# Weights of the seven-product tiles 64 bytes further in their places, sums of activations back at byte 0, in a two-block float32 kernel

## The reference

```python
    u = rms_norm(h, g_mlp) @ w_ff1                 # 1024 -> 4096
    h = h + jnp.square(jax.nn.relu(u)) @ w_ff2     # 4096 -> 1024
```

## Time and profile before

| what | us |
|---|---|
| median of three timed runs | 2050.3 (2049.81 to 2050.95) |
| the profiled execution, its own time | 2047.93 |
| its span, first to last instruction | 2046.1 |
| TensorE busy | 1995.9 (98% of the span) |
| GpSimd busy | 990.6 (48%) |
| VectorE busy | 1353.9 (66%) |
| ScalarE busy | 924.9 (45%) |

### The profile page before, as it was taken

How to read it: one execution, slowest core, us unless ns; L and a number is a source line. 1 busy time by engine, 2 the same in 40 slices (tenths; PEclk the granted TensorE clock), 3 DMA queues, 4 the chain that set the end, 5 groups by cost and what they waited for, 6 DMA issues and landing times.

```text
span 2046.1 us, 28723 instructions
## 1 busy us (share of the span) xinstructions
PE 1995.9 (98%) x11012; PEld 1598.4 (78%) x11012; DVE 1353.9 (66%) x2302; ACT 924.9 (45%) x1533; POOL 990.6 (48%) x1205
## 2 busy tenths in 40 slices
PE   6999999999999999999999999999999999999998
PEld 3877676888888667668889898786776788898877
DVE  5366758988294579966766565466896585665634
ACT  4542434443232556784333333445578533333342
POOL 1344204876666325541567767302345147676740
PEclk9999999999999999999999999999999999999999
DMA  9034631332333211113232324322111313323331
GB/s 330 28 105 142 220 124 43 103 102 83 106 101 103 77 54 42 45 39 104 75 111 83 117 90 134 97 75 80 46 42 42 103 63 103 103 85 122 114 103 62
DMA packets 166809, 194.43 MB, mean 95 GB/s; under 512 B 8592, under 2 KB 159504, under 8 KB 163216
## 3 DMA queue, kind: packets, MB, share of 16 engines
q1 hardware_dynamic: 166096, 189.44, 27.8%
q10 hardware_dynamic: 576, 3.15, 0.4%
HBM read 190.48 MB, written 2.10 MB: 94 GB/s over the span
## 4 chain that ended last, share of the span: by engine, by line
PE 67%; DVE 18%; ACT 5%; POOL 4%; DMA 4%; issue 2%; SPq 0%; DVEq 0%; ACTq 0%; POOLq 0%
PE ps L865 12%; PE ps L867 12%; PE ps L866 12%; POOL wl L3069 3%; DMA ring<-in_ff_seven_dram 3%; PE ps L884 2%; PE ps L886 2%; PE ps L885 2%; PE ps L1305 2%; PE ps L1307 2%; PE ps L1306 2%; PE ps L912 2%; DVE mix L2697 2%; DVE acts L2699 2%; ACT wh L1542 2%
## 5 line engine op out<-in xcount | busy, mean ns | idle before, releaser
L3069 POOL TENSOR_TENSOR wl<-ring,wh 128x256 fp32r<-128x256 f32 x1008 | 781.4, 810 | 592.3 <-ACT wh L1542 591.5
L1542 ACT ACTIVATE wh<-ring 128x1024 fp32r<-128x1024 f32 (+3 forms) x394 | 338.4, 888 | 305.7 <-DMA ring<-in_ff_seven_dram 93.5
L865 PE MATMUL ps<-acts,wh 128*128 128x512 f32 x880 | 345.6, 393 | 1.8 <-POOL wl L3069 1.2
L867 PE MATMUL ps<-acts,wl 128*128 128x512 f32 x880 | 342.7, 389 | 0.0
L866 PE MATMUL ps<-acts,wh 128*128 128x512 f32 x880 | 342.5, 389 | 0.0
L865 PE MATMUL ps<-xh,wh 128*128 128x512 f32 (+1 forms) x592 | 233.8, 395 | 2.6 <-POOL wl L3069 2.6
L2625 DVE SCALAR_TENSOR_TENSOR mix<-ps,par,mix 128x441 f32<-128x441 f32 (+2 forms) x352 | 213.8, 686 | 29.2 <-ACT mix L1789 29.1
L866 PE MATMUL ps<-xl,wh 128*128 128x512 f32 (+1 forms) x592 | 231.2, 391 | 0.0
L867 PE MATMUL ps<-xh,wl 128*128 128x512 f32 (+1 forms) x592 | 231.2, 391 | 0.0
L865 PEld LDWEIGHTS ps<-acts,wh 128*128 128x128 f32 x880 | 165.1, 188 | 40.9 <-issue 5.4
L867 PEld LDWEIGHTS ps<-acts,wl 128*128 128x128 f32 x880 | 165.2, 188 | 34.9
(11 more groups left out here) (474 smaller groups left out, 4133.6 us busy)
## 6 DMA issues: line engine op xcount, KB each, us to landing
ring<-in_w_ff_dram SPq DMA_DIRECT2D x40, 1024.0 KB, 5.2
ring<-in_w_in_dram SPq DMA_DIRECT2D x28, 1024.0 KB, 5.1
ring<-in_ff_seven_dram SPq DMA_DIRECT2D x24, 1024.0 KB, 4.8
ring<-in_ffn_w_up_dram SPq DMA_DIRECT2D x22, 1024.0 KB, 4.9
ring<-in_w_ada_dram SPq DMA_DIRECT2D x17, 1024.0 KB, 5.0
ring<-in_w_out_dram SPq DMA_DIRECT2D x12, 1024.0 KB, 5.1
ring<-in_ffn_w_down_dram SPq DMA_DIRECT2D x8, 1024.0 KB, 5.0
ring<-in_w_ple_gate_dram SPq DMA_DIRECT2D x8, 1024.0 KB, 5.0
```

Source lines behind the costliest of these rows:

```text
L865: t.matmul(b[0:m, 0:n], s.hi[:, k, a:a + m], x2[0][:, k, :], start=k == ks[0], stop=False)
L867: i = t.matmul(b[0:m, 0:n], s.lo[:, k, a:a + m], x2[0][:, k, :], start=False, stop=k == ks[-1])
L1542: a.activation(s.high[hf], s.raw[hf], ACT.Copy).then_inc(*up("hi", "hi", name, hf))
L3069: i = p.tensor_tensor(lo, raw, hi.bitcast(F32), ALU.subtract)
```

## The change

The split weights of seven-product tiles begin 16 elements (64 bytes) into their places, in `wh` and in `wl`, which grow by 16 elements. All four sums of activations begin at multiples of 128 bytes. `spots` now tells the planner that a part at place 3 of a seven-product tile also takes place 4 (its last 16 elements reach into it). Small tiles (`mod`, `rope`, `eps`, `posi`) move into the gaps behind `wh` and `wl`, `turn` moves up above the arenas, and four unused tiles pad the gaps, so that everything from `mix` on keeps its address; `h`, `xh`, `xl` and `wh` lie 1024 bytes lower, `wl` 512 bytes lower. No instruction is added or taken away.

```diff
+SEVEN_OFF = 16
...
-            self.hi, self.lo = [[x[:, 512 * q:512 * q + 512] for q in self.places] for x in (wh, wl)]
+            self.hi, self.lo = [[x[:, 512 * q + SEVEN_OFF:512 * q + SEVEN_OFF + 512] for q in self.places] for x in (wh, wl)]
...
     def spots(self, p):
 
-        return [(self.places[p], q) for q in range(2)] if self.seven else [(q, p) for q in self.places]
+        if not self.seven:
+            return [(q, p) for q in self.places]
+        q = self.places[p]
+        return [(q + i, u) for i in range(2 if q == 3 else 1) for u in range(2)]
...
-        con, par, rb, mod = sb("con", cn), sb("par", pn), sb("rb", rn), sb("mod", 96)
-        fw, pw, posi = sb("fw", 128), sb("pw", 128), sb("posi", 4, I32)
-        rope, eps, csil_t, small = sb("rope", 64), sb("eps", 3), sb("csil", 256), sb("small", 1024)
-        turn_t = sb("turn", 108)
+        con, par, rb = sb("con", cn), sb("par", pn), sb("rb", rn)
+        fw, pw, csil_t, small = sb("fw", 128), sb("pw", 128), sb("csil", 256), sb("small", 1024)
+        sb("beneath", 32)
         h_t, xh_t, xl_t = sb("h", 4096), sb("xh", 4096, F32R), sb("xl", 4096, F32R)
-        wh_t, wl_t = sb("wh", 2 * SLOT, F32R), sb("wl", 2 * SLOT, F32R)
+        wh_t, mod = sb("wh", 2 * SLOT + SEVEN_OFF, F32R), sb("mod", 96)
+        sb("between", 16)
+        wl_t, rope, eps, posi = sb("wl", 2 * SLOT + SEVEN_OFF, F32R), sb("rope", 64), sb("eps", 3), sb("posi", 4, I32)
+        sb("behind", 32)
+        with ExitStack() as low:
+            sb("ahead1", 28160, where=low)
+            turn_t = sb("turn", 108, where=low)
...
-                    sum1, sum2 = [sb(f"sum{i}{l}", 2160, F32R, where=high)[:, o:] for i, o in ((1, 16), (2, 0))]
+                    sum1, sum2 = [sb(f"sum{i}{l}", 2048, F32R, where=high) for i in (1, 2)]
```

## The result

The changed kernel takes **2089.97 us** (median of five runs, 2086.14 to 2091.4), the kernel before, timed beside it, 2050.3 us (2049.72 to 2050.95). The ratio is 1.0185, 95% interval 1.0174 to 1.0196: **slower, by 38 us by the ratio, 39.7 between the medians**. I had said 2089.0, in a range of 2070 to 2104.

A forecast was written before the change was run, and what follows sets the result against it. TensorE was taken to bound the kernel, with GpSimd and the load loop exactly in time. Twelve odd tiles at 3.3 us (39.6) less 0.7 for addresses gave +39 on 2050.3: 2089 us, range 2070 to 2104.

The forecast's parts named there:

- part (a): Odd tiles: part 3 also waits for place 4's old ff2 tile, is split later, product 3 starts 0.35 us late.
- (b): Odd tiles: part 4's split must wait for product 3 to end, so product 4 starts 1.75 us later still.
- GpSimd's queue: Odd tiles, before ff2: eight GpSimd instructions of 0.71 us behind part 4 make TensorE wait 1.2 us.
- rival 3: Waiting costs more than its length: GpSimd meets VectorE (23 us more, 2112) or TensorE's clock falls; chance 0.13 for both.
- Nothing given back: Odd tiles: the next load also goes out 3.3 us late, so the loop behind it shifts and recovers nothing.
- Rival 2: Odd tiles: GpSimd catches up or other waits are partly hidden; 1.7 to 2.5 us each, 2070 to 2080; chance 0.15.
- Rival 3's clock: TensorE's clock drops to half after waiting; at every odd tile 20 us, 2109; shares the chance of 0.13.
- The addresses: Seven-product matmuls: relative position of weights and activations counts, 1.41 not 1.44 us a product; only 0.7 us arrives.

The follow-up runs named there:

- kernel 2: Changed kernel, but part 3 of an odd tile waits for holders of places 3 and 4 and then holds only place 3: 2058.51 us, ratio 1.0056.
- kernel 4: Changed kernel with the low part of product 5 made by VectorE instead of GpSimd in all 24 tiles: 2073.53 us, ratio 1.0117.
- kernel 3: Changed kernel with the hold also at place 7 (such a part also holds place 0), so even tiles chain parts 3 and 4: 2125.08 us, ratio 1.0368.
- kernel 5: Changed kernel with sum1 and sum2 back at 64 bytes past a multiple of 128: 2085.63 us (one run).
- kernel 10: Changed kernel with the first four parts of odd tiles at the start of their places and the old `spots`: 2049.38 us, ratio 0.9999.
- kernel 6: Changed kernel with plain tiles' split weights also 64 bytes in, so nothing crosses, and the old `spots`: 2072.29 us, ratio 1.0118.
- kernel 7: Seven-product weights 64 bytes in as in the changed kernel, places 4 to 7 another 128 bytes higher, old `spots`: 2068.67 us, ratio 1.0096.
- kernel 9: Kernel before with only h, xh and xl moved 128 bytes lower (`turn` moved out of their way): 2058.97 us, ratio 1.0046.
- kernel 1: Kernel before with only the new `spots` rule, every address as before: 2087.83 us, ratio 1.0194.
- kernel 8: As kernel 7, but with the seven-product weights 32 bytes in instead of 64: 2070.01 us (one run).

## Why the prediction was right

**The planner, part (a).** Predicted: product 3 late by 0.35 us, its start 4.65 after the tile's (1080.5 - 1075.85). The row shows 4.63 (1087.63 - 1083.00), some 0.4 late. By itself, without (b), it is 0.85 (kernel 2): a part of its price is hidden by (b), since (b) takes VectorE's split away from beside GpSimd. I added the two terms as if they were independent. In the sum it made no error, because I had worked through the tile with both in place.

**Part (b), the direct wait.** Predicted 1.75, measured 3.06 - 1.41 = 1.65 in 12 odd tiles. Each link came from a row and held: high part 4 at 6.28 after the tile's start (I had 1082.2 - 1075.85 = 6.35), low part 0.66 behind it (0.67), product 4 at 7.69 (7.8).

**GpSimd's queue.** Predicted 1.2, measured 1.17 idle before ff2, which starts 13.23 after the tile's start (I had 13.4). The ten instructions took 0.70 each (I had 0.71 from the earlier trace rows), so rival 3's meeting with VectorE did not come in this stretch. It came in kernel 2, where VectorE splits at the same time. The Trainium skill, in SBUF — State Buffer, section Who interferes with whom, says that a VectorE instruction with two inputs in SBUF contends with a GpSimd one that reads SBUF; the run agrees, 1.25 us against 0.72.

**Nothing given back.** The load was to go out 3.3 us later; it went out 3.25 later (10.41 against 7.16). Rival 2, GpSimd catching up, needs this slack, and kernel 4, where GpSimd has two instructions less ahead of ff2, shows what it would have been worth: 1.05 us an odd round, 2073.53 us in all, inside the 2070 to 2080 that I gave this rival.

**The sum.** 12 x 3.3 = 39.6 was measured as 37.2 in the odd rounds: 0.2 us less in each, since ff2 starts 13.23 us after the tile and not 13.4. The first rounds of a layer, which I left out, lost 0.9 together, to a stretch at half clock. The two such stretches ahead of the rounds, some 3.4 us, belong to no term of mine and fill up the profiled span; that the median came within 1 us of mine is partly luck, and the fastest of the five runs, 2086.14 us, is the one with the highest mean granted clock (0.998).

**Rival 3's clock.** In the odd tiles it did not come: beside waits of 1.45 and 1.17 us the granted clock stayed at 1.00. But I had also argued against it with the first tile of a layer, whose 2.23 us of waiting left the clock at 1.00 in the kernel before. That argument was weak: in the changed kernel, with about the same waiting, it fell in one of the two first tiles, and in kernel 3 in both.

**The addresses.** The relative position counts, as I chose (kernel 5). Of the 0.7 us that I let arrive nothing can be seen in the total of the changed kernel, whose even rounds sum to 211.3 against 211.2: there the products are cheaper, but ff2 starts 1.65 us after product 6 (median) instead of 1.53, late again. In kernels 2 and 10 the gain does come, most even rounds at 21.0 to 21.05 against 21.1. From the independent read ports of the Trainium skill (SBUF — State Buffer, section Who interferes with whom) I had worked out a term of 0 for any address; kernels 6, 7 and 9, with 9 to 24 us for addresses alone, contradict that, well beyond the 3 us that I had in view. They do not show that a port waits.

**What I did not see.** In the expectations of kernels 6 and 7 I let an offset only save or do nothing for the reads of 512-column matmuls. Had I sorted those of the kernel before by where their two operands start, I would have seen that all that multiply split weights with xh, xl or acts have equal starts modulo 512 bytes. So its trace could not show what an unequal start costs, and I should have bounded that from both sides.

## What to carry to other kernels

When a layout change makes buffers touch their neighbours, read what the scheduler concludes from it before counting nanoseconds of access: 64 bytes of overlap cost one dependency between two parts of the same tile, and that moved work for three engines behind TensorE's own product, 3.1 us a tile against a gain of at most 0.15. If work has to go after the product that frees its place, its price is the whole chain to the first consumer plus everything queued behind it on the slowest helper. And an address rule found with one shape must be tried on the others, because it can reverse.

## What the runs showed of the hardware that I had not expected

- **Moving operand and weights, relative start.** Matmuls of 256 columns stand 120 ns apart with equal starts modulo 512 bytes, or with 128 bytes between them (product 3 of kernel 5), and 118 with 64 bytes between them, whichever of the two is shifted. Matmuls of 512 columns are the other way: 227 ns at equal starts throughout, 232 to 235 (medians) at a distance of 64, 128, 256 or 384 bytes, whichever of the two is shifted (kernels 6, 7, 9). In kernel 7 some with equal starts of their own are slow too. The kernels give the cost, not the cause.
- **A second, faster rhythm.** 256-column matmuls with the 64 bytes between them at times run 113.5 ns apart: in the odd tile above product 5 takes 1.36 us, product 0 takes 1.41, both at a granted clock of 1.00, on equal shapes and offsets. It often begins after a wait of TensorE, but a wait is neither enough (product 5 of most odd tiles of kernel 2 takes 1.41) nor needed (in kernel 6 whole tiles, as the one at 1110.8, run at 1.36 us a product with nothing waited for). In kernel 1, with its starts as before and after the same waits, product 5 takes 1.44. What starts it was not tried.
- **Half clock that comes and goes.** Stretches of 3.4 us at 0.50, at 1.2 instead of 2.4 GHz, appear in different number in kernels whose code there is the same. The first tile of layer 1 has one in the changed kernel and in kernels 1, 2, 3 and 10 and none in the kernel before and in kernels 4 to 9. In the changed kernel TensorE was busy for 1.68 of the 4.0 us before it; in the kernel before it was busy for 1.83 of 4.0 us at the same place (from 1686.5), and the clock stayed at 1.00. Two such stretches more or fewer are some 3.4 us, as much as the whole address effect that the change was about.
